# Two fused transformer blocks on one core: an earlier expert slot, filters first, and rotation work spread over the softmax

## What is computed

```python
def first_block(...):
    mod = (c @ w_ada[l] + b_ada[l])[:, None, :]            # 6 vectors of 1024
    sh1, sc1, gt1, sh2, sc2, gt2 = jnp.split(mod, 6, axis=-1)
    h = rms_norm(x, g_mix[l]) * (1 + sc1) + sh1
    p = h @ w_in[l] + b_in[l]
    q, k, v, o, gates, hx = jnp.split(p, split_pts, axis=-1)
    y_m = mlstm_mixer(q, k, v, o, gates, ...)
    filt = hyena_filters(...)      # two sine layers of 64, then @ w3, times exp(-t |delta|) + 0.05
    y_h = hyena_mixer(hx, ..., filt, ...)                  # long convolutions by spectra
    x = x + gt1 * (jnp.concatenate([y_m, y_h], -1) @ w_out[l])
    hf = rms_norm(x, g_ffn[l]) * (1 + sc2) + sh2
    x = x + gt2 * expert_choice_moe(hf, w_router[l], w_gate[l], w_up[l], w_down[l])
    return rms_norm(x, g_final)

def expert_choice_moe(xn, ...):    # each of 16 experts takes its 32 best tokens
    aff = jax.nn.softmax(xn @ w_router, axis=-1)
    g, idx = lax.top_k(jnp.swapaxes(aff, 1, 2), cap)
    xs = xn[bidx, idx]
    hid = silu(xs @ w_gate[e]) * (xs @ w_up[e])            # 1024 -> 2048, each expert
    return zeros.at[bidx, idx].add((hid @ w_down[e]) * g)

# second block, each of two layers: modulation; neighbourhood attention (6 heads),
# gated linear attention (4 heads), grouped-query attention (6 heads) with
apply_axial_rope(rms_norm_2(heads, w), cos, sin)           # xf * cos + rot * sin
gla_output(o, norm_w, g)                                   # rms_norm_2(o) * silu(g)
# then @ w_out, layer norm, SwiGLU with 2816 hidden, layer norm
```

## Time and profile before

| | |
|---|---|
| median of 3 runs | 2398.76 us (2394.21 to 2399.8) |
| the profiled execution | 2396.77 us, span of its instructions 2395.0 us |
| TensorE matmul busy | 2074.6 us (87%), mean granted clock 0.953 |
| VectorE, ScalarE, GpSimd busy | 547.4, 403.7, 185.1 us |
| moved by DMA | 664 MB, 277 GB/s over the span |

### The profile page before, as it was taken

One profiled execution on the slowest core, in us unless ns is written; L12 is line 12 of the kernel. 1 busy time (PEld: TensorE's weight loads), 2 busy tenths in 40 slices (PEclk: granted clock), 3 DMA queues, 4 the chain that ended last, 5 costly groups with the idle time before them and its releaser, 6 DMA issues. The chain is left out here.

```text
span 2395.0 us, 32997 instructions
## 1 busy us (share of the span) xinstructions
PE 2074.6 (87%) x14348; PEld 1437.3 (60%) x14348; DVE 547.4 (23%) x1182; ACT 403.7 (17%) x737; POOL 185.1 (8%) x182
## 2 busy tenths in 40 slices
PE   6998888888687888898789786997999999899997
PEld 2674455554244545665356442674888877478886
DVE  3433433010342200000000210346300024522001
ACT  1122002021131200000000220336200023431001
POOL 0025000000100000000000000026000002420000
PEclk8999898999899999998999999998999999899999
DMA  9459757999999999999999999630344642124450
GB/s 371 166 212 376 291 189 309 412 408 414 421 408 405 418 415 414 420 420 414 415 412 426 421 412 417 179 107 1 124 158 141 155 168 99 44 71 141 135 159 23
DMA packets 206791, 664.03 MB, mean 277 GB/s; under 512 B 18359, under 2 KB 129368, under 8 KB 164344
## 3 DMA queue, kind: packets, MB, share of 16 engines
q1 hardware_dynamic: 206648, 661.93, 71.4%
HBM read 660.86 MB, written 1.05 MB: 276 GB/s over the span
## 5 line engine op out<-in xcount | busy, mean ns | idle before, releaser
L1046 PE MATMUL ps<-arena,ring 128*128 128x256 f32 x2240 | 484.8, 379 | 3.2 <-DVEq L370 3.2
L1046 PEld LDWEIGHTS ps<-arena,ring 128*128 128x128 f32 x2240 | 425.3, 190 | 62.5 <-DVEq L370 4.8
L609 PE MATMUL ps<-arena,ring 128*128 128x256 f32 (+2 forms) x1552 | 349.1, 385 | 14.8 <-DMA ring<-in_w_ffn_in 8.8
L1393 PE MATMUL ps<-ring,arena 128*32 128x256 f32 x4032 | 260.5, 405 | 85.9 <-DMA ring<-in_w_up 54.0
L609 PEld LDWEIGHTS ps<-arena,ring 128*128 128x128 f32 (+2 forms) x1552 | 275.2, 183 | 94.6 <-issue 22.4
L1393 PEld LDWEIGHTS ps<-ring,arena 128*32 128x32 f32 x4032 | 126.2, 115 | 207.7 <-DMA ring<-in_w_up 70.5
L1419 PE MATMUL ps<-ring,arena 128*32 128x512 f32 x1024 | 142.1, 679 | 78.5 <-DMA ring<-in_w_down 74.1
L1968 ACT ACTIVATE arena<-ps 128x512 f32<-128x512 f32 (+3 forms) x137 | 74.8, 546 | 770.1 <-PE ps L609 406.0
L1419 PEld LDWEIGHTS ps<-ring,arena 128*32 128x32 f32 x1024 | 29.5, 116 | 170.4 <-DMA ring<-in_w_down 113.9
L1119 PE MATMUL ps<-arena,ring 128*128 128x256 f32 x512 | 113.6, 383 | 5.0 <-issue 5.0
L1119 PEld LDWEIGHTS ps<-arena,ring 128*128 128x128 f32 x512 | 98.1, 192 | 22.3 <-issue 9.0
(11 more groups left out here) (339 smaller groups left out, 1771.4 us busy)
## 6 DMA issues: line engine op xcount, KB each, us to landing
ring<-in_w_up SPq DMA_DIRECT2D x64, 2048.0 KB, 13.8
ring<-in_w_down SPq DMA_DIRECT2D x64, 2048.0 KB, 14.6
ring<-in_w_gate SPq DMA_DIRECT2D x62, 2048.0 KB, 13.1
ring<-in_w_ada SPq DMA_DIRECT2D x36, 2048.0 KB, 12.0
ring<-in_w_ffn_in SPq DMA_DIRECT2D x64, 1024.0 KB, 7.9
ring<-in_w_ffn_out SPq DMA_DIRECT2D x16, 1408.0 KB, 7.0
ring<-in_w_in SPq DMA_DIRECT2D x9, 2048.0 KB, 9.0
ring<-in_w_out SPq DMA_DIRECT2D x6, 2048.0 KB, 7.8
```

The costliest lines, as they stand in the source:

```text
L609: m = mm(o, a, x, start=(k == 0 and r == 0), stop=(k == kt - 1 and last))
L1046: m = mm(b, w[:, k, c:c + P], src[:, k, :], start=(k == 0), stop=(k == kt - 1))
L1393: m = mm(b[u][32 * c:32 * c + 32, T * x:T * x + T], xs[:, 2 * h + k, CAP * e:CAP * e + CAP], w[:, k, at_:at_ + T], start=(h == 0 and k == ...
```

## The change

Three edits. In the stream, entry `n_before + 6` (up0_1) gets a place of its own at 12312 of the arena, where the mixer's output `yT` lay, and SyncE's wait for the chosen tokens and the tables move behind it; ahead of it stands a wait for `ht_ready` 4 (h copied by token). At the start, the small inputs, tables, deltas and x are issued ahead of all modulation slots; the engines make the filters with one ada step between the two orders, one after `ss0` and three between the spectra of the two orders; x is squared on GpSimd; h is made in three passes (x by reciprocal root, then scale and shift, four tiles on VectorE and four on ScalarE); the window has two buffers. In the latent softmax the three sine products of the rotation are made ahead of round 0, the other passes after rounds 0 and 1, and the reciprocals and gate passes after rounds 2, 3 and 4. Some semaphores that were implied by others are gone.

```diff
-        win = at(23600, W)
+        win = [at(23600, W), at(25136, W)]
-        rtmp = at(7152, 2, T)
+        rtmp = [at(7152, 2, T), at(8944, T), at(8432, 2, T)]
-        early = {n_before: 16424, n_before + 1: 20520}
+        early = {n_before: 16424, n_before + 1: 20520, n_before + 6: 12312}
@@ tensor
-            pe.wait_ge(s_fil, 96)
+            pe.wait_ge(s_hid, 48)
             b = open_bank(pe, "hid1", MIX_BANKS)
             close_bank(mm(b[0:64, 0:T], hw1[0:33, :], hfe[0:33, :], start=True, stop=True), "hid1")
-            ada1()
+            pe.wait_ge(s_fil, 48)
             pe.wait_ge(hid_ready, 1)
             b = open_bank(pe, "hid2", MIX_BANKS)
             close_bank(mm(b[0:64, 0:T], hw2[0:64, :], hid[0:64, :], start=True, stop=True), "hid2")
-            pe.wait_ge(s_load, 32)
-            ada1()
...
-                    if 2 * o + n < 3:
-                        ada1()
-            sums("ss0", sq0, 1)
-            for o in range(2):
+                if o == 0:
+                    ada1()
+            pe.wait_ge(s_load, 32)
+            sums("ss0", sq0, sq0_ready)
+            ada1()
+
+            def spectrum(o):
...
+            spectrum(0)
+            ada1(3)
+            spectrum(1)
...
             pe.wait_ge(h_ready, 1)
+            pe.wait_ge(ht_scaled, 1)
             project("q")
@@ scalar
-                        if k:
-                            act.wait_ge(win_used, k)
-                        step(a(win, dlt[:, W * j:W * j + W], ACT.Exp, scale=tb("minus_t")[:, n:n + 1]), win_ready)
-                    if 2 * o + n < 3:
-                        ada1()
+                        if k > 1:
+                            act.wait_ge(win_used, k - 1)
+                        step(a(win[d], dlt[:, W * j:W * j + W], ACT.Exp, scale=tb("minus_t")[:, n:n + 1]), win_ready)
...
             root("ss0", rs, T, 0)
+            ada1(5)
+            act.wait_ge(a1_ready, 1)
+            for m in range(4, KD):
+                step(a(hT[:, m, :], hT[:, m, :], ACT.Identity, scale=A1[:, m:m + 1], bias=mod[:, m:m + 1]))
+            tell(ht_scaled)
@@ vector
-            dve.wait_ge(s_fil, 96)
-            step(v.tensor_copy(cpad[:, :, 0], pc("c", 0, 8)), c_ready)
+            dve.wait_ge(s_hid, 48)
...
+                if i == 0:
+                    dve.wait_ge(s_fil, 48)
+                    step(v.tensor_copy(cpad[:, :, 0], pc("c", 0, 8)), c_ready)
...
-            dve.wait_ge(s_x, 16)
-            step(tt(sq0, xT, xT, ALU.mult), sq_ready)
...
-            modulated(dve, step, tell, pc("g_mix", 0, 8), mod[:, 8:16], mod[:, 0:8], 1, xT)
-            for o in range(2):
+            dve.wait_ge(s_x, 16)
+            dve.wait_ge(root_ready, 1)
+            step(v.reciprocal(rs, rs))
+            for m in range(KD):
+                step(tt(hT[:, m, :], xT[:, m, :], rs, ALU.mult))
+
+            def spectrum(o):
...
+            spectrum(0)
+            ada1(5)
+            step(stt(out=A1, in0=mod[:, 8:16], scalar=1.0, in1=pc("g_mix", 0, 8), op0=ALU.add, op1=ALU.mult))
+            tell(a1_ready)
+            for m in range(4):
+                step(ts(hT[:, m, :], hT[:, m, :], A1[:, m:m + 1], mod[:, m:m + 1], ALU.mult, ALU.add))
+            tell(h_ready)
+            spectrum(1)
@@ vector, latent layers
+            def rotations(N):
+
+                for i in range(3):
+                    b = read_bank(dve, f"rot{i}{N}")
+                    if i == 1:
+                        step(tt(rtmp[i], b[:, 0:T], tb2("rope_s"), ALU.mult), frees=f"rot{i}{N}")
+                    else:
+                        step(tt(rtmp[i], b[:].rearrange("p (c t) -> p c t", c=2), bc(tb2("rope_s"), 1, 2, T), ALU.mult), frees=f"rot{i}{N}")
+
+            def rotated(i):
+                x = (gaq[:, 0:2, :], gaq[:, 2, :], gak[:, :, T:2 * T])[i]
+                step(tt(x, x, tb2("rope_c") if i == 1 else bc(tb2("rope_c"), 1, 2, T), ALU.mult))
+                step(tt(x, x, rtmp[i], ALU.add))
+                if i == 2:
+                    tell(rope_ready)
...
                 gla_out(X, N)
+                rotations(N)
...
                     if j == 0:
-                        rotated(l, N)
+                        rotated(0)
                     if j == 1:
-                        gla_normed(X, 1 + l, l)
+                        rotated(1)
+                        rotated(2)
+                    if j in (2, 3):
+                        if j == 2:
+                            dve.wait_ge(oroot_ready, 2 + l)
+                        step(v.reciprocal(grt[:, j - 2, :], grt[:, j - 2, :]))
+                    if j == 4:
+                        step(stt(out=og[X], in0=og[X], scalar=pc(f"gla_norm_{l}"), in1=grt, op0=ALU.mult, op1=ALU.mult))
+                        step(tt(oT[X][:, 3:5, :], og[X], glg, ALU.mult))
@@ gpsimd
+            pool.wait_ge(s_x, 16)
+            step(g.tensor_tensor(sq0, xT, xT, ALU.mult), sq0_ready)
             pool.wait_ge(s_load, 32)
-            pool.wait_ge(pad_ready, 1)
@@ sync
+            sp.dma_start(tab[:], I["tables1"]).then_inc(s_load, 16)
+            sp.dma_start(dlt, I["hy_deltas"].to_broadcast([P, 4 * W])).then_inc(s_load, 16)
+            sp.dma_start(xT, I["xT"].rearrange("(k p) t -> p k t", p=P)).then_inc(s_x, 16)
...
-                if n == 0:
-                    sp.dma_start(tab[:], I["tables1"]).then_inc(s_load, 16)
-                    sp.dma_start(dlt, I["hy_deltas"].to_broadcast([P, 4 * W])).then_inc(s_load, 16)
-                if n == 2:
-                    sp.dma_start(xT, I["xT"].rearrange("(k p) t -> p k t", p=P)).then_inc(s_x, 16)
...
                 if n == n_before + 6:
+                    sp.wait_ge(ht_ready, 4)
+                if n == n_before + 7:
                     sp.wait_ge(xs_ready, 8)
```

More of the change, by code:

```diff
@@ L376, in build @@
         s_load = sem("tables_loaded")
+        s_hid = sem("filter_features_loaded")
         s_fil = sem("filter_inputs_loaded")
+        sq0_ready, a1_ready, ht_scaled = sem("x_squares_ready"), sem("scale_ready"), sem("h_second_half_ready")
         s_row = sem("rows_loaded")
@@ L1158, in _, with sums @@
             ada1, ada2 = ada_steps(ADA1, ada_rows, ada_turn), ada_steps(ADA2, ada_rows, ada_turn)
-            def sums(name, src, count):
-                pe.wait_ge(sq_ready, count)
+            def sums(name, src, ready):
+                pe.wait_ge(ready, 1)
                 b = open_bank(pe, name, MIX_BANKS)
@@ L1335, in _ @@
                 release_with(f"mix{2 * j + 1}")
-            sums("ss1", T1v, 2)
+            sums("ss1", T1v, sq_ready)
             ada2(3)
@@ L1625, in modulated @@
             T1v = T1.rearrange("p (a b) -> p a b", b=T)
-            if k != 1:
-                step(tt(T1v, src, src, ALU.mult), sq_ready)
-            if k == 3:
-                read_bank(dve, "col_ada0_2")
+            step(tt(T1v, src, src, ALU.mult), sq_ready)
+            read_bank(dve, "col_ada0_2")
             step(stt(out=A1, in0=scale, scalar=1.0, in1=gain, op0=ALU.add, op1=ALU.mult))
@@ L1685, in dve_mixers @@
                         dve.wait_ge(win_ready, k + 1)
-                        step(stt(out=hwt[:, d, :], in0=win, scalar=0.05, in1=b[:], op0=ALU.add, op1=ALU.mult), frees=name)
+                        step(stt(out=hwt[:, d, :], in0=win[d], scalar=0.05, in1=b[:], op0=ALU.add, op1=ALU.mult), frees=name)
                         tell(win_used)
@@ L1710, in dve_mixers @@
                     step(v.memset(pad[:, :, e:e + 1], 0.0))
-            tell(pad_ready)
             def conv(dst, src, wname, bname, m, n):
@@ L1734, in dve_mixers @@
                      frees=f"v{t}")
-            tell(v_ready)
             ada1()
@@ L2099, in context @@
                 N = "c0"
[L2100 removed]
+                act.wait_ge(ab_ready, 1)
                 for k in range(KD):
@@ L2347, in head_normed @@
                     tell(gnorm_ready[st])
-            def rotated(l, N):
-                for i, x in enumerate((gaq[:, 0:2, :], gaq[:, 2, :], gak[:, :, T:2 * T])):
+            def rotations(N):
+                for i in range(3):
                     b = read_bank(dve, f"rot{i}{N}")
                     if i == 1:
-                        src, tmp, co, si = b[:, 0:T], rtmp[:, 0, :], tb2("rope_c"), tb2("rope_s")
+                        step(tt(rtmp[i], b[:, 0:T], tb2("rope_s"), ALU.mult), frees=f"rot{i}{N}")
                     else:
-                        src, tmp = b[:].rearrange("p (c t) -> p c t", c=2), rtmp
-                        co, si = bc(tb2("rope_c"), 1, 2, T), bc(tb2("rope_s"), 1, 2, T)
-                    step(tt(tmp, src, si, ALU.mult), frees=f"rot{i}{N}")
-                    step(tt(x, x, co, ALU.mult))
-                    step(tt(x, x, tmp, ALU.add))
-                tell(rope_ready)
+                        step(tt(rtmp[i], b[:].rearrange("p (c t) -> p c t", c=2), bc(tb2("rope_s"), 1, 2, T), ALU.mult), frees=f"rot{i}{N}")
[5 more added lines that the diff above has]
+                    tell(rope_ready)
```

(2 more changed lines are left out.)

20 lines of the change are left out of this document (6 added, 14 removed).

## The result

The changed kernel takes 2378.97 us (median of 4 runs, 2374.17 to 2386.32) beside 2396.65 us for the kernel before (median of 4 runs); the ratio is 0.9926 with a 95% interval of 0.9905 to 0.9946. Run again beside 22 runs of before (median 2394.02; one of them took 4181.46 us and is left out of the ratio), it gave 2377.16 us, ratio 0.9922 (0.9908 to 0.9937). The forecast was 2377 with a range of 2368 to 2388, so time and range hold. The sum behind it was 21.8 us, and 17 to 19 were measured. The profiled execution of the changed kernel, whose rows follow, took 2386.32 us (span 2383.8), the longest of its four; it is read for where the work lies, and sizes are taken from all traces together.

What follows compares the result with a forecast made beforehand. TensorE was taken to bound 60 to 180 us and 1700 to 2000, transfers 413 to 1500. Start 9.0, slot 5.1 and softmax 7.7 sum to 21.8 off the 2398.76 median: 2377 us, range 2368 to 2388.

Steps and rivals of the forecast that it cites:

- The sum behind it: Whole kernel: 9.0 from the start, 5.1 from the seventh slot, 7.7 from the latent softmax, together 21.8 us saved.
- The start: Before the projections: reordered loads and TensorE work bring `project("q")` from 70.94 to 61.6; 9.0 us taken.
- step 0: Start: the first modulation step runs when ada0 lands at 22.0, takes 3.64 us and ends at 25.6.
- `ss0`: Start: TensorE's sum of squares of x, behind the order 1 filters, takes 5.41 us and ends at 35.0.
- The slot: Expert stream: up0_1, issued early, takes 2.10 MB out of the DMA-bound stage at 414 GB/s; 5.1 us.
- The end of the stage: Expert stage, a sign to look for: the last w_down wait comes 14 us earlier.
- The softmax: Latent layers: moving rotation and gate passes off one stretch of VectorE work saves 3.9 us a layer, 7.7 for two.
- the four periods behind the first: Latent softmax: periods after the fifth maximum are 6.34 plus added pieces: 8.7, 8.0, 8.0, 7.8, 32.6 in all against 32.1 before.
- rival D: Latent softmax: moved VectorE passes contend with GpSimd, about 4 a layer by 0.4, 3 us in all, 2380; chance 0.09.
- each of four periods 0.5 longer: Latent softmax, lower bound: if the periods run that much over the forecast, the gain is 1.9 us a layer.
- Rival B: Latent softmax: loop stays as long because VectorE work shifts maxima in four periods; gain 0 to 1 a layer, 2384; chance 0.12.
- the 0.62 us of waiting is all there is: Latent softmax: VectorE's only idle time per period, so no sign the four pieces are wholly covered (8.7 a layer).

Runs made afterwards that it cites:

- products: Changed kernel plus extra TensorE matrix products, result unread, before the second filter layer, first filters and first modulation step; 2376.57 us, ratio 0.9914.
- the products in the loop: Changed kernel plus three TensorE matrix products, result unread, in round 0 of the latent softmax; 2376.25 us, ratio 0.9916.
- the slot alone: Kernel before with only up0_1's own arena place and the moved wait for chosen tokens; 2388.26 us, ratio 0.9976.
- both moves: Changed kernel with all rotations finished before the first softmax maximum and the whole gate normalization in the last round; 2366.02 us, ratio 0.9873.

## Why the prediction was right, and where it was not

**The total.** The forecast of 2377 came within 2 us partly by luck. The sum was 3 to 5 us too large, and the median of before from which it was taken away, 2398.76 of three runs, came out as 2396.65 with the fourth.

**The start, 9.0 forecast.** Right: 9.6 to 11 us alone. Over the seven traces with the changed start and neither products nor loads changed at it, q begins at 61.9 on average and at 70.3 in the three with the old one, 8.4 earlier. At the issue of the tables, 398.8 after 405.7 in the same traces, 6.9 of that are left. Two terms were off and canceled: step 0 began 1.4 us later than 22.0, since ada0 landed later, and in the fast executions `ss0` took 3.72 instead of 5.41. Not foreseen was that the same order can run 5.2 us slower in some executions (q at 65.93 and, with the products in the loop, 65.70) and that gates and v can run at half clock behind a fast start (1.9 us of the first execution's 10.2 were gone when the tables were issued).

**The slot, 5.1 forecast.** Right: 5.8 by the median of the slot alone, 5.9 by the stages. The price of a slot in a stage bound by transfers came out as its bytes over the measured rate. By the 358 GB/s that the Trainium skill gives for HBM to one core (SBUF — State Buffer, A bandwidth-pool intuition that's wrong) the estimate had been 5.9; the measured values, 4.8 to 5.9, don't tell 5.1 from 5.9, while the rate itself is 413 over the expert stage, so the agreement is no proof of that figure. The end of the stage was to come 14 us earlier: the first transfer issued behind it (in_rpb) came 10.0 and 14.6 earlier in the two executions.

**The softmax, 7.7 forecast, 2.4 measured.** The step that failed is the line of the four periods behind the first. That a piece adds to a round all but the short wait was read rightly; what the periods are besides was taken from one period without pieces and at full clock, and came out too small. In the first layer: first distance 7.14 (7.85 expected, that is 12.26 less 4.4), then 9.45, 8.99, 8.11, 8.16 against 8.7, 8.0, 8.0, 7.8. So 34.7 where 32.6 stood (those four add up to 32.5), and 2.6 us gained instead of 3.9. In the second layer the four are 35.4. (From the earlier trace rows the last reciprocal ends 6.30 behind the first maximum, and the wait is 0.66, not 6.34 and 0.62; that changes nothing.) The second layer gained nothing. It has two lengths in either kernel, by whether TensorE's first scores ran at full clock: the old softmax took 73.1 in two traces and 71.48 in one, the changed one 73.5 in two and 71.6 to 71.8 in three. What was missing:

- In the second layer the second distance ends with a wait of 0.42 for scores and the third holds one of 1.32 (the maxima of 2062.73 and 2065.85), since TensorE computes them at half clock (2.08 us a group instead of 1.13) after its wait. I had taken the scores as always there. With no rotation in that round the second distance is still 9.14 in the second layer, against 7.60 in the first.
- The passes with two inputs in SBUF are longer under GpSimd: 0.80 instead of 0.42 for a 128x256, 0.98 instead of 0.69 for the product with the gate. That is rival D, at 0.4 plus 0.3 in the first layer and 0.3 more in the second, not 1.5. Against before it is less still: the old loop paid 0.37 and 0.3 in its first layer (1.06 and 0.72 for two of its sums) and nothing in its second. That such a pair contends is what the Trainium skill states (SBUF — State Buffer, Who interferes with whom), and the trace agrees.
- In the second layer the tail grew from 14.60 to 15.8 us: in the chain that ended last, eight transposes took 1.94 us and the products by the values behind them 2.51, where others take 1.09 and 1.95. The granted clock from 2095 to 2099 us was 0.57.

The bound "each of four periods 0.5 longer" (1.9 a layer) held for the first layer alone. Rival B, gain 0 to 1 a layer, is what the second layer did.

**The step before all that.** The prediction said "the 0.62 us of waiting is all there is", and drew its sum from it, but not the consequence: if a piece is covered for 0.6 us at most in any round, spreading it can win no more than that a round, and what pays is to take it out. By this reading the spread's gain comes from the three sine products that left the loop (no run moved these alone); both moves took the other pieces out and gained 11.5 us more.

## What to carry to other kernels

In a loop in which four engines hand one unit around, read the slack of one period before placing work in it: here some 0.6 us of 6.97, so a piece of 1.75 us cost 1.2 in its round (8.12 and 8.16 after 6.97), while in the tail, where VectorE had 3.5 us to wait, the gate's whole 5.1 us cost about 1.5. A slot moved out of a stage bound by transfers is worth its bytes at the stage's own rate, and a start read as one serial list of row durations came out within 2.1 us in the five executions whose filters of order 1 ran fast, two errors in it canceling, and some 4 us short in the two others. When executions scatter by 5 us, compare stretches of the traces and not totals.

## What the runs showed of the hardware

- A VectorE pass with two SBUF inputs ended only after a GpSimd pass over SBUF that had begun ahead of it. The sum of two filters, 0.69 us elsewhere, took 3.17 here and ended 0.55 us after GpSimd's square of x (GpSimd, then VectorE, start and length; 3.25 in two other executions, which also ended 0.54 and 0.55 us after it):

```profile
18.40 3.60 POOL L2722 TENSOR_TENSOR arena<-XC 128x2048 f32<-128x2048 f32 x1 [17.98 <-DMA XC<-in_xT]
...
19.38 3.17 DVE L1690 TENSOR_TENSOR arena<-arena 128x512 f32<-128x512 f32 x1
```

- With the changed start TensorE's first products ran at half speed until at least 24 us in all ten traces, and until 38 to 39 us in three, idle between them or not. The filters of order 1 took 3.70 us in four of these traces, 3.77 to 4.36 in three and 7.19 in three, and in two executions of the same kernel 3.70 and 7.19; nothing before them tells these apart. The column of the granted clock reads 1.00 over that time, where the trace has no record of it.
- In the first execution of the changed kernel the granted clock fell to 0.50 (1.2 GHz) from 95 to 101.9 us, although TensorE had been busy 5.00 us of the 5 before and was busy throughout; in the second execution, with the same work, it was 1.00.
- The expert stage, bound by transfers, varies by 8 us between executions of kernels that are equal there (1104.2 to 1112.5, on four sets of runs; 1104.2 to 1110.1 on one chip).
